# Recurrence of a two-layer hybrid block: turned strict part and turned inverse as 128x128 tiles with anti-diagonal blocks

## The reference, cut to what matters

```python
def step(s, inp):
    r_t, w_t, k_t, v_t, a_t, b_t = inp
    sa = jnp.einsum('bhvk,bhk->bhv', s, a_t)
    s = s * w_t[:, :, None, :] + sa[..., None] * b_t[:, :, None, :] + v_t[..., None] * k_t[:, :, None, :]
    y = jnp.einsum('bhvk,bhk->bhv', s, r_t) if emit else None
    return s, y
```

## Time and profile before

| what | value |
|---|---|
| median of 3 runs | 2888.08 us (2887.6 to 2889.34) |
| span of the profiled execution (first to last instruction) | 2891.8 us |
| TensorE (PE) busy | 2785.9 us, 96% |
| VectorE (DVE) busy | 1191.4 us, 41% |
| ScalarE (ACT) busy | 685.4 us, 24% |
| mean granted TensorE clock | 0.991 |

### The profile page before, as it was taken

How to read it: one execution, slowest core, us unless ns; L and a number is a source line. 1 busy time by engine, 2 the same in 40 slices (tenths; PEclk the granted TensorE clock), 3 DMA queues, 4 the chain that set the end, 5 groups by cost and what they waited for, 6 DMA issues and landing times.

```text
span 2891.8 us, 63838 instructions
## 1 busy us (share of the span) xinstructions
PE 2785.9 (96%) x29030; PEld 1672.3 (58%) x29030; DVE 1191.4 (41%) x2524; ACT 685.4 (24%) x1425; POOL 3.0 (0%) x7
## 2 busy tenths in 40 slices
PE   7999999999999999999998999989999999999997
PEld 4467777445777888864577787863333333333332
DVE  4777565444546444237786564431111011011101
ACT  2345312544322111013454126520000000000000
POOL 0000000000000000000000000000000000000000
PEclk9999999999999999999999999999999999999999
DMA  7100143212232433232000442459999999999995
GB/s 293 59 3 4 47 148 122 66 44 84 91 127 78 146 117 90 80 120 84 30 4 5 168 160 96 148 218 348 413 364 365 415 359 378 400 364 412 364 379 199
DMA packets 188786, 534.55 MB, mean 185 GB/s; under 512 B 6112, under 2 KB 80096, under 8 KB 171104
## 3 DMA queue, kind: packets, MB, share of 16 engines
q1 hardware_dynamic: 187440, 526.21, 48.5%
q0 software_dynamic: 1072, 4.19, 0.4%
HBM read 528.29 MB, written 2.10 MB: 183 GB/s over the span
## 4 chain that ended last, share of the span: by engine, by line
PE 92%; DVE 3%; ACT 2%; issue 1%; SPq 1%; DMA 0%; DVEq 0%; ACTq 0%
PE bank L583 68%; PE bank L711 12%; PE bank L1357 8%; PE bank L829 2%; PE bank L1219 1%; SPq L3014 1%; ACT WR L1647 1%; DMA rep<-in_repeated 0%; ACT ar L1647 0%; PE bank L948 0%; DVE WR L2480 0%; DVE RS L2351 0%; PE bank L1519 0%; DVE ar L2410 0%; ACT L1647 0%
## 5 line engine op out<-in xcount | busy, mean ns | idle before, releaser
L583 PE MATMUL bank<-AT,WR 128*128 128x512 f32 (+1 forms) x1408 | 519.9, 519 | 6.3 <-ACT AT L1647 3.7
L1647 ACT ACTIVATE ar<-bank 128x256 f32<-128x256 f32 (+2 forms) x338 | 155.1, 463 | 1533.4 <-PE bank L583 1026.5
L583 PE MATMUL bank<-WR,ar 128*32 128x512 f32 (+1 forms) x4464 | 444.5, 555 | 1.6 <-DVE ar L2923 1.6
L583 PE MATMUL bank<-ar 128*32 128x512 f32 (+6 forms) x3990 | 429.6, 509 | 9.7 <-ACT ar L1647 5.7
L583 PEld LDWEIGHTS bank<-AT,WR 128*128 128x128 f32 x1408 | 262.4, 191 | 212.5 <-issue 196.4
L583 PEld LDWEIGHTS bank<-ar 128*32 128x32 f32 (+3 forms) x3990 | 176.1, 124 | 248.3 <-issue 236.4
L583 PEld LDWEIGHTS bank<-WR,ar 128*32 128x32 f32 x4464 | 143.7, 110 | 288.4 <-issue 285.8
L1647 ACT ACTIVATE WR<-bank 128x512 f32<-128x512 f32 (+1 forms) x224 | 125.1, 593 | 200.2 <-PE bank L583 166.7
L583 PE MATMUL bank<-AT,ar 128*32 128x512 f32 (+1 forms) x1456 | 151.4, 561 | 11.9 <-ACT AT L1647 11.9
L2933 DVE TENSOR_TENSOR YB<-YB,bank 128x512 f32<-128x512 f32 x28 | 18.0, 684 | 343.3 <-PE bank L583 343.3
L2941 DVE TENSOR_TENSOR ar<-ar,bank 128x512 f32<-128x512 f32 (+1 forms) x48 | 29.8, 621 | 286.5 <-PE bank L583 285.1
(11 more groups left out here) (368 smaller groups left out, 3296.6 us busy)
## 6 DMA issues: line engine op xcount, KB each, us to landing
WR<-in_moe_w_down SPq DMA_DIRECT2D x27, 2048.0 KB, 15.2
WR<-in_ada_w SPq DMA_DIRECT2D x20, 2048.0 KB, 8.2
ar<-in_moe_w_down SPq DMA_DIRECT2D x20, 2048.0 KB, 14.7
WR<-in_w_in SPq DMA_DIRECT2D x18, 2048.0 KB, 8.9
WR<-in_moe_w_gate SPq DMA_DIRECT2D x18, 2048.0 KB, 17.0
WR<-in_moe_w_up SPq DMA_DIRECT2D x15, 2048.0 KB, 16.2
WR<-in_moe_w_up SPq DMA_DIRECT2D x18, 1536.0 KB, 7.8
WR<-in_moe_w_gate SPq DMA_DIRECT2D x15, 1536.0 KB, 9.1
```

The source lines that it names most:

```text
L583: return pe.matmul(o, lhsT, rhs, start=first, stop=last)
L1647: return act.activation(out, in_, func, **k)
```

## The change

- The turned strict part is kept in one tile `LB` of 128 x 8 x 128, two 64x64 blocks per q on the anti-diagonal; between them, the other two blocks are zero. `level` is then one product with 128x128 weights and 64 columns per q, instead of two of 64x64. The swap of halves comes with it.
- The turned inverse `XT` is kept in the same way, as two tiles of that form (one for the start, one for all n). Growth is one such product per q, and so is `solve`. The turned products stay 64x64, two per q, right behind the growth product of the same q.
- Values and Gram products no longer stand beside a level; they are issued behind it (`gram_ahead`, and a loop over `value_turned`).
- ScalarE copies each turned product in two halves of 64 partitions into the blocks (`turned_in`). VectorE fills the two tiles of a chunk's start with four `copy_predicated`, in place of one and a product with a mask. At the start of a layer it sets up the new tiles.

The core of the diff:

```diff
-    masks.append(two(lambda d: (r // 2 == c // 2) & later[d](c, r) | (r == c)))
+    masks.append(two(lambda d: (r // 2 == c // 2) & later[d](c, r)))
...
-        LTs = [HTf[:, 3072 + 512 * b:3584 + 512 * b] for b in range(2)]
+        LB = HTf[:, 3072:4096].rearrange("p (q w) -> p q w", q=8)
...
-                    [x2[:, 512 * n:512 * n + 512] for n in (1, 0)], [x2[:, 512 * n:512 * n + 512] for n in (3, 2, 6)],
+                    [x2[:, 512 * n:512 * n + 512] for n in (1, 0)],
+                    [x2[:, a:a + 1024].rearrange("p (q w) -> p q w", q=8) for a in (1024, 3072)],
...
-                def solve(i, q, h):
-                    last = mm(pair(solved_bank, q, 1 - h), pair(XT[2], q, 1 - h), pair(G, q, 1 - h), True, True)
-                    if q == 7:
-                        last.then_inc(A.full, 1)
+                def solve(i):
+                    pe.wait_ge(A.free, A.jobs[("XT", l, i, 4)])
+                    for q in range(8):
+                        cols = slice(64 * q, 64 * q + 64)
+                        last = mm(solved_bank[:, cols], XT[1][:, q, :], G[:, cols], True, True)
+                    last.then_inc(A.full, 2)
+                    for h in range(2):
                         A.done(("U", l, i, h))

                 def gram(i, what, bank, q, h):
                     ba, aa = BK[i % 2][64 * h:64 * h + 64, q, 0:64], pair(MV[:, i % 2, 0, :], q, h)
-                    return mm(pair(bank, q, h), *((aa, ba) if what == "X" else (ba, aa)), True, True)
-
-                def level(i, n, beside=None):
+                    if what == "X":
+                        return mm(pair(bank, q, h), aa, ba, True, True)
+                    return mm(pair(bank, q, 1 - h), ba, aa, True, True)
+
+                def gram_ahead(i, what):
+                    if what == "X":
+                        pe.wait_ge(operands_ready, seen(operands_ready))
+                        pe.wait_ge(A.free, A.jobs[("vt", l, i - 1, 1)])
+                    else:
+                        pe.wait_ge(S.free, S.jobs[("gram", l, i, "X")])
+                    for q, h in hq:
+                        last = gram(i, what, gram_bank, q, h)
+                    last.then_inc(S.full, 1)
+                    S.done(("gram", l, i, what))
+
+                def level(i, n):
                     if n:
                         pe.wait_ge(A.free, A.jobs[("X", l, i, n - 1)])
                     else:
-                        pe.wait_ge(inverse_ready, seen(inverse_ready))
+                        pe.wait_ge(inverse_ready, seen(inverse_ready, 2))
...
                         if i:
                             pe.wait_ge(A.free, A.jobs[("G", l, i - 1)])
-                    if beside == "solve":
-                        pe.wait_ge(A.free, A.jobs[("XT", l, i - 1, 4)])
-                    if beside == "X":
-                        pe.wait_ge(operands_ready, seen(operands_ready))
-                        pe.wait_ge(A.free, A.jobs[("vt", l, i, 1)])
-                    if beside == "LT":
-                        pe.wait_ge(S.free, S.jobs[("gram", l, i + 1, "X")])
                     for q in range(8):
                         bank = level_banks(i, n)[q // 4]
-                        for h in range(2):
-                            ins = mm(pair(bank, q, 1 - h if n else h), pair(LTs[i % 2], q, h), pair(X[n > 0], q, h), True, True)
+                        ins = mm(bank[:, 64 * q:64 * q + 64], LB[:, q, :], X[n > 0][:, 64 * q:64 * q + 64], True, True)
                         if q % 4 == 3:
                             ins.then_inc(S.full, 1)
                             S.done(("T1", l, i, n, q // 4))
-                        for h in range(2 if beside else 0):
-                            if beside == "solve":
-                                solve(i - 1, q, h)
-                            elif beside == "values":
-                                value_turned(i, q, h)
-                            else:
-                                last = gram(i + 1, beside, gram_bank, q, h)
-                    if beside in ("X", "LT"):
-                        last.then_inc(S.full, 1)
-                        S.done(("gram", l, i + 1, beside))

                 def inverse_doubled(i, n):
-                    x, t1 = (swapped(XT[1]), swapped(T1)) if n else (compact(XT[0]), compact(T1))
+                    x, t1 = XT[n > 0], swapped(T1)
                     if n:
                         pe.wait_ge(A.free, A.jobs[("XT", l, i, n - 1)])
                     elif i:
...
                         if q % 4 == 0:
                             pe.wait_ge(S.free, S.jobs[("T1", l, i, n, q // 4)])
                         if n < 4:
-                            for h in range(2):
-                                ins = mm(pair(grown_bank(i, n), q, h), x(q, h), t1(q, h), True, True)
-                                if (q, h) == (7, 1):
-                                    ins.then_inc(A.full, 1)
+                            cols = slice(64 * q, 64 * q + 64)
+                            ins = mm(grown_bank(i, n)[:, cols], x[:, q, :], T1[:, cols], True, True)
+                            if q == 7:
+                                ins.then_inc(A.full, 1)
                         for h in range(2):
-                            last = mm(pair(turned_bank(i, n), q, 1 - h), t1(q, h), x(q, h), True, True)
+                            turned = x[64 - 64 * h:128 - 64 * h, q, 64 * h:64 * h + 64]
+                            last = mm(pair(turned_bank(i, n), q, 1 - h), t1(q, h), turned, True, True)
                     last.then_inc(A.full, 1)
...
                 for i in range(NCH):
                     if i:
                         level(i, 0)
-                        pe.wait_ge(A.free, A.jobs[("XT", l, i - 1, 4)])
-                        for q, h in hq:
-                            solve(i - 1, q, h)
+                        solve(i - 1)
                         inverse_doubled(i, 0)
                         y_of_chunk(i - 1, ybank)
                         level(i, 1)
...
                         inverse_doubled(i, 1)
                         if i <= 4:
                             bonus(i - 1)
-                        level(i, 2, "values")
+                        level(i, 2)
+                        for q, h in hq:
+                            value_turned(i, q, h)
                         pe.wait_ge(responses_ready, seen(responses_ready))
                         against(i, 0)
                         inverse_doubled(i, 2)
                         against(i, 2)
-                    level(i, 3, "X" if i < NCH - 1 else None)
+                    level(i, 3)
+                    if i < NCH - 1:
+                        gram_ahead(i + 1, "X")
                     against(i, 4)
                     inverse_doubled(i, 3)
                     against(i, 6)
-                    level(i, 4, "LT" if i < NCH - 1 else None)
+                    level(i, 4)
+                    if i < NCH - 1:
+                        gram_ahead(i + 1, "LT")
                     if i == 0:
                         pe.wait_ge(uv_cleared, seen(uv_cleared))
                     ybank = from_state(i)
                     inverse_doubled(i, 4)
-                pe.wait_ge(A.free, A.jobs[("XT", l, NCH - 1, 4)])
-                for q, h in hq:
-                    solve(NCH - 1, q, h)
+                solve(NCH - 1)
                 y_of_chunk(NCH - 1, ybank)
...
+                def turned_in(bank):
+                    A.take()
+                    act.wait_ge(A.full, A.taken)
+                    for h in range(2):
+                        rows = slice(64 - 64 * h, 128 - 64 * h)
+                        ins = f(XT[1][rows, :, 64 * h:64 * h + 64], bank[rows, :].rearrange("p (q w) -> p q w", q=8), ACT.Copy)
+                        if h:
+                            free(ins)
+
                 for d in range(2):
                     decays(l, 1, d)
                 for i in range(NCH):
                     for n in range(5):
                         if n == 0 and i:
-                            stacked_in(slice(0, 64), solved_bank, 1)
+                            stacked_in(slice(0, 64), solved_bank, 0)
                         if n == 2:
                             stacked_in(slice(64, 128), gram_bank, 0)
                         if n < 4:
                             copied(X[1], grown_bank(i, n))
                         else:
                             copied(G, grown_bank(i, n))
-                        copied(XT[1 + n // 4], turned_bank(i, n))
+                        turned_in(turned_bank(i, n))
...

-                    LT = LTs[i % 2]
-                    dve.copy_predicated(dq(LT), mk(M_STRICT_T).bitcast(u32), step_product(bank)).then_inc(S.free, 1)
-                    dve.wait_ge(S.free, S.taken)
-                    v(TT(dq(XT[0]), dq(LT), mk(M_PAIR_T), ALU.mult), inverse_ready, wait=False)
+                    S.take()
+                    dve.wait_ge(S.full, S.taken)
```

(18 more changed lines are left out.)

## The result

The changed kernel takes 3550.43 us (median; 3532.39 to 3578.42), the kernel before 2888.24: ratio 1.2292, 95% interval 1.2228 to 1.2357, +662 us. I had forecast 3215 and a range up to 3265. The page of the changed kernel (of the run that took 3536.48 us): span, busy time, PE's clock in 40 slices, the chain.

The account below looks back on a forecast made before the run. PE's work in the recurrence loops was taken as the bound: +344 us of PE work, +3 for tile setup, -20 of idle time make +327, 3219 profiled, 3215 us as median; range 3130 to 3265.

Parts of the forecast that it names:

- What bounds the kernel: In the recurrence loops PE's own work is the bound; at most 37 us can be won by better overlap.
- Levels and solutions: 80 levels and 16 solutions, each 1.79 us as large products instead of 0.93: +69 and +14 us.
- The bound from two sides: Large MATMUL with 64 columns priced from neighbours with 3 and 128 columns: 0.112 us each, 1.79 for sixteen.
- Companions, tiles and copies, idle time: 42 value and Gram groups behind levels +39 us; layer-start tiles +3, other copies covered; PE idle time won back -20.
- The doublings, at the full clock: 64 growth steps with turned products, 0.55 us per q, 4.4 us instead of 0.93 each: +222 us.
- the first rival: Doublings: no drain when shapes alternate quickly, 0.34 us per q; 3108 us in all, chance 0.10.
- The clock: Rival: gaps of 0.09 us in doublings bring 1.2 GHz, doubling their 282 us; about 3497 us, chance 0.04.
- PE's clock still at 1.00 in the loops: Sign in the profile after that would show the forecast right: PE at full clock in the recurrence loops.
- No drain at quick alternation: Rival: next weights load while the last product streams, doubling 2.73 us; 3108 us in all, chance 0.10.
- The ACT chain: Rival: second halves of ACT's turned copies come late in each of 80 steps, +48 us: 3263, chance 0.05.
- Time by the number of instructions: Rival: removing 2560 MATMULs from the loops saves 71 us, "issue" waits some 12 more: 2805 us, chance 0.02.

Follow-up runs that it names:

- growth_small: The changed kernel with the growth products alone back at 64x64, levels and solutions still 128x128: 2986.86 us, ratio 1.0327.
- all_small: The changed kernel with every product back at 64x64, its new tiles, copies and order otherwise kept: 2905.85 us, ratio 1.0045.
- companions_behind: The kernel before with one edit, values and Gram products behind their level instead of beside it: 2896.35 us, ratio 1.003.
- grain_two: The changed kernel with each doubling in four parts, two large growth products then four small turned ones: 3153.78 us, ratio 1.0922.
- growth_then_turned: The changed kernel with all eight large growth products of a doubling first, then all sixteen small turned ones: 3095.12 us, ratio 1.0698.
- wide: The changed kernel with large growth and level products streaming 128 columns instead of 64 for six of eight q: 3249.54 us, ratio 1.1253.
- growth_large_only: The changed kernel with levels and solutions back at 64x64, growth still 128x128: 3249.39 us, ratio 1.1236.
- wide_levels: The changed kernel with only the level products streaming 128 columns for six of eight q: 3341.44 us, ratio 1.1553.

## Why the prediction was wrong

**What bounds the kernel** held: PE's work, and nothing else came forward.

**Levels and solutions**: 69 + 14 = 83 us forecast, 81 measured (growth_small against all_small). The bound from two sides (3 and 128 columns, 0.11 us each) was right for 64: 1.84 us per group where I had 1.79.

**Companions, tiles and copies, idle time**: 39 + 3 - 20 = 22 us forecast, 13 measured (all_small). The term of 39 was too large: by itself it adds 23 us to PE's busy time, and 7 us to the kernel's (companions_behind). In the changed kernel PE is idle 3.4 of 484 and 5.5 of 510 us, so of the 37 us of the earlier trace rows 28 were won back, where I had taken 20.

**The doublings, at the full clock**: 222 us forecast; 5.01 - 1.09 = 3.92 us each, 251 us, measured. I had set my 4.4 against 0.93, which leaves out the way out of the small doubling. The mechanism was right, that each change of shape drains the engine, and each q pays for two of them. The size was off: 0.63 us per q, above the upper bound of 0.58. A round trip costs 0.29 us by the rows (0.31 by grain_two's time) on top of unmixed work. My 0.52 to 0.58 for each q held only 0.18 to 0.24 for it, over the 0.34 of the first rival, although I had read 0.34 for a whole round trip in the earlier trace rows. The sum at the full clock is 13 + 81 + 251 = 345 us, 3233; the other ways above give 3223 to 3234. I had said 3215, so everything but the clock makes an error of 10 to 20 us. On the drain the Trainium skill (TensorEngine Tiling (Array Packing), Key Properties) agrees: a change of tiling mode drains the engine.

**The clock** is the step that failed: the sum prices every term at full speed and puts the clock's cost at nothing, and "PE's clock still at 1.00 in the loops" stood among the signs of being right. Measured were 0.67 and 0.62, and some 320 us. I gave the fall 4 in 100 with the words "Against it: the gaps are fifty times shorter". I had read one fall in the trace before, after 4.54 us without a MATMUL, and took idle time of that length for the only cause. The same trace has others that I did not look at. One lies within layer 1's loop, after 1.74 us without a MATMUL; PE's timeline and the window behind it (length; busy of PE, PEld, DVE, ACT, POOL; clock; DMA):

```profile
1579.98 0.97 PE L829 MATMUL bank<-WR 128*64 128x64 f32 x25 [1.74 <-issue]
```

```profile
1581.50:1584.90 3.40, 3.40 (x72) 3.40 (x68) 0.85 (x2) 0.69 (x2) 0.00 (x0) 0.50 0.00 0
```

So a pause of 4.5 us was no condition even there. The runs with large products showed falls in stretches in which PE is busy 100% by the profile. The price I named, 64 x 4.4 = 282 us and 3497 in all, was near what it cost, 3550 - 3230 = some 320 us, half of the whole loss. That was luck: at 1.2 GHz a doubling takes 8.22 instead of 5.01 us, not twice as long, and not all of them ran there, so all 64 could have lost 205 us at most. The rest was lost by the levels (3.60 for 1.93) and the loops' other products, which I had left at full speed. That the lower clock follows from how the array is used in the loops, and not from waits, is shown: the same products in runs of eight keep 0.99 (growth_then_turned), and the same products in the same order with 128 columns in each large one keep 0.99 too (wide). Both parts share in it: with either the levels small (growth_large_only, 92 us of clock) or the levels wide (wide_levels, about 110) the fall is much less deep. What of a product the chip counts, these runs don't tell.

**The rivals.** No drain at quick alternation: out; it wanted 2.73 us for a doubling, and each round trip costs the same 0.29 us up to eight. The ACT chain: out; PE waits 3.4 us for anything in layer 0's loop. Time by the number of instructions (2805 us): out, with 5120 fewer instructions on PE and its loads the kernel is 23% slower. The Trainium skill (TensorEngine Tiling (Array Packing), Instruction Overhead) speaks of some 60 cycles for each matmul. No run here shows that as the limit: a large f32 MATMUL costs 0.11 us for 3, 64 or 128 columns. That its weight load sets this pace fits the loads of the earlier trace rows, but no run tested it.

## What to carry to other kernels

Two 64x64 products on separate quarters of the array cost 0.058 us per slot, one zero-padded 128x128 product of the same f32 operands 0.11 per MATMUL: halving the number of products doubled the time. Keep products of one tile shape together; each there-and-back between 128x128 and 64x64 took 0.29 us here, and cutting one loop over q in two was worth 455 us. Compare durations that end the same way: a group with the way out into another shape is longer than one without. When a change makes products short and broken up, ask for the granted clock in the windows of the stretch, not for PE's busy share, and give a fall of it a real chance in the forecast.

## What the runs showed of the hardware that I had not expected

- The granted clock stood at 1.2 GHz for 58 us on end (264.9 to 322.8) while PE was busy 57.90 of 57.90 us by the profile.
- More work in the same instructions made the kernel faster: 128 columns per large product in place of 64 (in six of eight) took it from 3550 to 3250 us, with the clock up from 0.89 to 0.99.
- MATMULs on other quarters of the array can start before ones issued earlier: Gram products issued behind the level started at 220.98, and the level's last at 221.14 (companions_behind).
- PE's waits of up to 1.5 us without a releaser in the kernel before (7.8 us of the earlier trace rows) went to 1.0 us in all when values and Gram products stood behind their level (companions_behind). Their cause was not tested.
